# The two long convolutions of each layer: transforms folded by token parity and by mirrored frequency

## What is computed

```python
def hyena_filters(L, w1, b1, w2, b2, w3, b3, freq, w_out, deltas):
    ...
    a = jnp.sin(freq * (a @ w3 + b3))
    decay = jnp.exp(-t * jnp.abs(deltas)[None, :])
    h = ((a @ w_out) * decay).astype(jnp.float32).reshape(L, N_DIRS, HYENA_ORDER, D_HYENA)
    fwd, bwd = h[:, 0], h[:, 1]
    two_sided = jnp.concatenate(
        [fwd, jnp.zeros((1, HYENA_ORDER, D_HYENA), jnp.float32), bwd[:0:-1]], axis=0)
    return jnp.fft.rfft(two_sided, axis=0)

def fft_long_conv(u, h_f, bias):
    L = u.shape[1]
    u32 = u.astype(jnp.float32)
    y = jnp.fft.irfft(jnp.fft.rfft(u32, n=2 * L, axis=1) * h_f[None], n=2 * L, axis=1)[:, :L]
    return (y + u32 * bias.astype(jnp.float32)).astype(u.dtype)
...
        z = fft_long_conv(hv, filt[:, 0], flt_bias[l, 0]) * hx1
        z = fft_long_conv(z, filt[:, 1], flt_bias[l, 1]) * hx2
        y_h = z * jax.nn.silu(z_h)
```

## Time and profile before

| | us |
|---|---|
| median of 3 runs (2068.70 to 2070.05) | 2069.11 |
| the profiled execution | 2067.41 |
| its span, first to last instruction | 2065.6 |
| TensorE busy in it | 1998.3 (97%) |
| VectorE busy | 659.8 (32%) |
| ScalarE busy | 379.0 (18%) |
| mean granted TensorE clock | 0.985 |

### The profile page before, as it was taken

The page is one execution under the profiler, slowest core; times in us unless marked ns, Lnnn a source line. Parts: engine busy times, 40 slices in busy tenths (PEclk is TensorE's granted clock), DMA queues, the critical chain, the costliest instruction groups (busy, mean ns, idle before and its releaser), DMA issues.

```text
span 2065.6 us, 28841 instructions
## 1 busy us (share of the span) xinstructions
PE 1998.3 (97%) x12128; PEld 1104.6 (53%) x12128; DVE 659.8 (32%) x1436; ACT 379.0 (18%) x784; POOL 111.1 (5%) x94
## 2 busy tenths in 40 slices
PE   6999999999998999999989988999999999999998
PEld 5577775667774865777756544232323333333332
DVE  3265113345212474344449934010101010111112
ACT  3212103212102232243320012010101010111101
POOL 0000000000000000000016610000000000000000
PEclk9999999999999999999999998999999999999999
DMA  8245575344665223243323125989898979797973
GB/s 316 82 163 204 217 282 202 116 156 171 234 265 228 82 82 150 115 175 131 123 102 123 41 102 217 376 329 374 324 384 330 381 309 403 311 402 298 406 299 148
DMA packets 41645, 472.71 MB, mean 229 GB/s; under 512 B 4676, under 2 KB 6340, under 8 KB 8040
## 3 DMA queue, kind: packets, MB, share of 16 engines
q1 hardware_dynamic: 39008, 465.44, 56.6%
q10 hardware_dynamic: 2568, 6.31, 0.9%
HBM read 470.68 MB, written 1.06 MB: 228 GB/s over the span
## 4 chain that ended last, share of the span: by engine, by line
PE 88%; DVE 7%; DMA 3%; issue 1%; ACT 0%; ACTq 0%; SPq 0%; POOLq 0%; POOL 0%; DVEq 0%
PE bank L898 21%; PE bank L551 14%; PE bank L928 11%; PE bank L850 7%; PE bank L862 3%; PE bank L714 3%; PE bank L543 3%; PE bank L536 3%; PE bank L720 3%; PE bank L564 2%; PE bank L978 2%; PE bank L970 2%; DMA arena<-in_wgu 1%; PE bank L617 1%; PE bank L649 1%; PE bank L1074 1%
## 5 line engine op out<-in xcount | busy, mean ns | idle before, releaser
L898 PE MATMUL bank<-arena 128*32 128x512 f32 x4096 | 453.1, 594 | 1.7 <-DMA arena<-in_wgu 1.7
L551 PE MATMUL bank<-arena 128*128 128x256 f32 x1408 | 312.6, 381 | 0.0
L898 PEld LDWEIGHTS bank<-arena 128*32 128x32 f32 x4096 | 130.3, 110 | 311.1 <-issue 296.3
L551 PEld LDWEIGHTS bank<-arena 128*128 128x128 f32 x1408 | 264.9, 190 | 53.7 <-issue 19.4
L928 PE MATMUL bank<-arena 128*32 128x512 f32 x2112 | 238.2, 595 | 0.0
L1993 DVE TENSOR_TENSOR arena<-arena,bank 128x256 f32<-128x256 f32 x64 | 27.0, 421 | 595.3 <-ACT arena L1406 540.4
L850 PE MATMUL bank<-arena 128*128 128x256 f32 x704 | 153.7, 379 | 0.1
L850 PEld LDWEIGHTS bank<-arena 128*128 128x128 f32 x704 | 133.6, 190 | 21.7 <-issue 4.1
L928 PEld LDWEIGHTS bank<-arena 128*32 128x32 f32 x2112 | 63.0, 110 | 133.2 <-issue 132.5
L1406 ACT ACTIVATE arena<-bank 128x256 f32<-128x256 f32 x64 | 24.5, 383 | 587.9 <-PE bank L898 587.9
L2207 POOL TENSOR_TENSOR arena<-arena 128x512 f32<-128x512 f32 x64 | 81.2, 1268 | 293.0 <-DVE arena L2040 290.5
(11 more groups left out here) (416 smaller groups left out, 1952.6 us busy)
## 6 DMA issues: line engine op xcount, KB each, us to landing
arena<-in_wgu SPq DMA_DIRECT2D x88, 2048.0 KB, 9.4
arena<-in_w SPq DMA_DIRECT2D x46, 2048.0 KB, 8.1
arena<-in_wdn SPq DMA_DIRECT2D x88, 1024.0 KB, 7.9
arena<-in_modw SPq DMA_DIRECT2D x24, 2048.0 KB, 10.2
arena<-in_wf SPq DMA_DIRECT2D x11, 3072.0 KB, 10.3
arena<-in_flt_deltas ACTq DMA_DIRECT2D x2, 1024.0 KB, 15.6
cst<-in_consts SPq DMA_DIRECT2D x1, 1162.0 KB, 17.3
arena<-in_x SPq DMA_DIRECT2D x1, 1024.0 KB, 5.3
```

The lines of the kernel that those rows point to most:

```text
L551: ins = mm(bank[b][:, j * S:(j + 1) * S], w[:, col:col + P], hT[:, k, :], start=(k == 0), stop=(k == KT - 1))
L898: ins = mm(bank[w % 2][32 * j:32 * j + 32, :], hTe[:, k, TOK * b:TOK * b + TOK], wslot[c % RING][:, k, :], start=(k == 0), stop=(k == KT - ...
```

## The change

Of the 256 frequencies only the lower 128 are transformed, once over the even tokens and once over the odd tokens. At the mirrored frequency the cosine of an even token is the same and that of an odd token has its sign turned, and the sine the other way round; so the upper half is a difference where the lower is a sum.

- The constants are reordered: rows of tokens by parity, and the inverse's rows mirrored. The decay's times, the columns of `fa` and of the transposes' source are taken with a step of two.
- "f_spec": 4 matmuls of 128x512 for each order, not 8. ScalarE copies two of the four banks, and VectorE makes sum and difference with the other two: 4 instructions for each order.
- "dft": 2 matmuls of 128x512 for each half, not 4; the second accumulates onto the first. ScalarE copies the first's two banks aside (`even`, signalled as du_ready), the matmuls of the second step wait for that and no longer for VectorE. VectorE does nothing in the first step; in the second it does both halves' six instructions, two that make the upper half (`2 * even - sum`), and four sums over `Y` for the inverse: 18 in a row.
- "idft": 16 matmuls of 128x128, not 128x256, with the constants read in steps of two elements; VectorE reads the bank de-interleaved.
- The table moves the "dft" steps behind "mix", and "turn" and "idft" of both orders one place later.
- Three waits are merged into others: filter_landed for delta_landed and fwo_landed, mask_landed for ffw_landed, ScalarE's own chain for two of its waits.

```diff
         7: [("dft", 0, 0), ("scores", 0, 0)],
-        8: [("dft", 0, 1), ("mix", 0, 0)],
-        9: [("weigh", 0, 0), ("idft", 0, 0), ("scores", 1, 0)],
-        10: [("turn", 1, 0), ("mix", 1, 0), ("values", 0, 0)],
-        11: [("weigh", 1, 0), ("dft", 1, 0), ("scores", 2, 0)],
-        12: [("dft", 1, 1), ("mix", 2, 0), ("values", 1, 0)],
-        13: [("weigh", 2, 0), ("scores", 3, 0)],
+        8: [("mix", 0, 0), ("dft", 0, 1)],
+        9: [("weigh", 0, 0), ("scores", 1, 0)],
+        10: [("mix", 1, 0), ("idft", 0, 0), ("values", 0, 0)],
+        11: [("weigh", 1, 0), ("turn", 1, 0), ("scores", 2, 0)],
+        12: [("mix", 2, 0), ("dft", 1, 0), ("values", 1, 0)],
+        13: [("weigh", 2, 0), ("dft", 1, 1), ("scores", 3, 0)],
         14: [("mix", 3, 0), ("values", 2, 0)],
-        15: [("weigh", 3, 0), ("idft", 1, 0)],
-        16: [("values", 3, 0)],
+        15: [("weigh", 3, 0)],
+        16: [("values", 3, 0), ("idft", 1, 0)],
...
                     elif name == "f_spec":
 
                         pe.wait_ge(sm["fold_ready"], l + 1)
-                        for kt in range(2):
+                        if c == 1:
+                            pe.wait_ge(sm["fp_done"], l * 4 + 2)
+                        for t in range(TT):
                             for ri in range(2):
-                                q = 2 * kt + ri
-                                if c == 1:
-                                    pe.wait_ge(sm["fp_done"], l * 8 + q + 1)
-                                for t in range(TT):
-                                    lhs = (FCt, FSt)[ri][:, t, kt * P:(kt + 1) * P]
-                                    rhs = hf[:, t, c, :] if ri == 0 else hn[:, t, c, :]
-                                    ins = mm(bank[4 + q][:, :], lhs, rhs, start=(t == 0), stop=(t == TT - 1))
-                                ins.then_inc(sm["fp_ps"], 1)
+                                src = (hf, hn)[ri][:, t, c, :]
+                                mm(bank[4 + 2 * t + ri][:, :], (FCt, FSt)[ri][:, t, 0:P], src,
+                                   start=True, stop=True).then_inc(sm["fp_ps"], 1)
...
                                 ins = nc.tensor.transpose(bank[2 + t][:, j * P:(j + 1) * P],
-                                                          src[:, j, t * P:(t + 1) * P], ident)
+                                                          src[:, j, t::2], ident)
...
 
                         if h == 0:
                             pe.wait_ge(sm["utok_ready"], l * 4 + 2 * c + 2)
                         else:
-                            pe.wait_ge(sm["spec_ready"], l * 4 + 2 * c + 1)
+                            pe.wait_ge(sm["du_ready"], l * 4 + 2 * c + 2)
                         for ri in range(2):
-                            for t in range(TT):
-                                ins = mm(bank[2 + ri][:, :], (FCt, FSt)[ri][:, t, h * P:(h + 1) * P], utok[:, t, :],
-                                         start=(t == 0), stop=(t == TT - 1))
+                            ins = mm(bank[2 + ri][:, :], (FCt, FSt)[ri][:, h, 0:P], utok[:, h, :],
+                                     start=(h == 0), stop=True, skip_group_check=True)
                         ins.then_inc(sm["dft_ps"], 1)
                     elif name == "idft":
 
                         pe.wait_ge(sm["spec_ready"], l * 4 + 2 * c + 2)
                         for j in range(4):
-                            for kt in range(2):
+                            for t in range(TT):
+                                at = (j % 2) * S + t * P
                                 for ri in range(2):
-                                    ins = mm(bank[2 + j // 2][:, (j % 2) * S:(j % 2 + 1) * S],
-                                             Y[:, kt, ri, j * P:(j + 1) * P], (FCk, FSk)[ri][:, kt, :],
-                                             start=(kt == 0 and ri == 0), stop=(kt == 1 and ri == 1))
+                                    ins = mm(bank[2 + j // 2][:, at:at + P], H[:, c, t, ri, j * P:(j + 1) * P],
+                                             (FCk, FSk)[ri][:, 0, t::2], start=(ri == 0), stop=(ri == 1))
...
-                        for q in range(4):
-                            act.wait_ge(sm["fp_ps"], l * 8 + 4 * c + q + 1)
-                            F(H[:, c, q // 2, q % 2, :], bank[4 + q][:, :], ACT.Copy).then_inc(sm["fp_done"], 1)
+                        for ri in range(2):
+                            act.wait_ge(sm["fp_ps"], l * 8 + 4 * c + ri + 1)
+                            F(H[:, c, 1, ri, :], bank[4 + ri][:, :], ACT.Copy).then_inc(sm["fh_ready"], 1)
+                    elif name == "dft" and h == 0:
+                        act.wait_ge(sm["dft_ps"], l * 4 + 2 * c + 1)
+                        for ri in range(2):
+                            F(even[:, ri, :], bank[2 + ri][:, :], ACT.Copy).then_inc(sm["du_ready"], 1)
...
-                        if c == 0 and h == 0:
-                            dve.wait_ge(sm["fp_done"], l * 8 + 8)
-                        dve.wait_ge(sm["dft_ps"], l * 4 + 2 * c + h + 1)
-                        C, Sn = bank[2][:, :], bank[3][:, :]
-                        re, im = H[:, c, h, 0, :], H[:, c, h, 1, :]
-                        link(v.tensor_tensor(tmp[:, 0, :], C, re, ALU.mult))
-                        link(v.tensor_tensor(tmp[:, 1, :], Sn, im, ALU.mult))
-                        link(v.tensor_tensor(Y[:, h, 0, :], tmp[:, 0, :], tmp[:, 1, :], ALU.add))
-                        link(v.tensor_tensor(tmp[:, 0, :], Sn, re, ALU.mult))
-                        link(v.tensor_tensor(tmp[:, 1, :], C, im, ALU.mult))
-                        v.tensor_tensor(Y[:, h, 1, :], tmp[:, 0, :], tmp[:, 1, :], ALU.subtract).then_inc(sm["spec_ready"], 1)
-                        dve.wait_ge(sm["spec_ready"], l * 4 + 2 * c + h + 1)
+                        if h == 0:
+                            continue
+                        dve.wait_ge(sm["du_ready"], l * 4 + 2 * c + 2)
+                        dve.wait_ge(sm["dft_ps"], l * 4 + 2 * c + 2)
+                        for half in range(2):
+                            re, im = H[:, c, half, 0, :], H[:, c, half, 1, :]
+                            if half == 0:
+                                C, Sn = bank[2][:, :], bank[3][:, :]
+                            else:
+
+                                C, Sn = even[:, 0, :], even[:, 1, :]
+                                link(v.scalar_tensor_tensor(C, C, 2.0, bank[2][:, :], ALU.mult, ALU.subtract))
+                                link(v.scalar_tensor_tensor(Sn, Sn, -2.0, bank[3][:, :], ALU.mult, ALU.add))
+                            link(v.tensor_tensor(tmp[:, 0, :], C, re, ALU.mult))
+                            link(v.tensor_tensor(tmp[:, 1, :], Sn, im, ALU.mult))
+                            link(v.tensor_tensor(Y[:, half, 0, :], tmp[:, 0, :], tmp[:, 1, :], ALU.add))
+                            link(v.tensor_tensor(tmp[:, 0, :], Sn, re, ALU.mult))
+                            link(v.tensor_tensor(tmp[:, 1, :], C, im, ALU.mult))
+                            link(v.tensor_tensor(Y[:, half, 1, :], tmp[:, 0, :], tmp[:, 1, :], ALU.subtract))
+                        for ri in range(2):
+                            for t in range(TT):
+                                ins = v.tensor_tensor(H[:, c, t, ri, :], Y[:, 0, ri, :], Y[:, 1, ri, :],
+                                                      ALU.add if ri == t else ALU.subtract)
+                                if t == 0:
+                                    link(ins)
+                            ins.then_inc(sm["spec_ready"], 1)
+                            dve.wait_ge(sm["spec_ready"], l * 4 + 2 * c + ri + 1)
+                    elif name == "f_spec":
+                        for ri in range(2):
+                            dve.wait_ge(sm["fh_ready"], l * 4 + 2 * c + ri + 1)
+                            dve.wait_ge(sm["fp_ps"], l * 8 + 4 * c + 2 + ri + 1)
+                            whole, alias, odd = H[:, c, 0, ri, :], H[:, c, 1, ri, :], bank[6 + ri][:, :]
+                            link(v.tensor_tensor(whole, alias, odd, ALU.add))
+                            ab = (alias, odd) if ri == 0 else (odd, alias)
+                            v.tensor_tensor(alias, ab[0], ab[1], ALU.subtract).then_inc(sm["fp_done"], 1)
+                            dve.wait_ge(sm["fp_done"], l * 4 + 2 * c + ri + 1)
                     elif name == "idft":
                         u, gate = (hvT, hx1T) if c == 0 else (hx1T, hx2T)
                         if c == 1:
@@ -1615,9 +1638,11 @@
                         for b in range(2):
                             dve.wait_ge(sm["idft_ps"], l * 4 + 2 * c + b + 1)
                             for j in (2 * b, 2 * b + 1):
-                                link(v.scalar_tensor_tensor(tmp[:, 0, 0:S], u[:, j, :],
+                                turned = bank[2 + b][:, (j % 2) * S:(j % 2 + 1) * S]
```

(9 more changed lines are left out.)

43 lines of the change are left out of this document (20 added, 23 removed).

## The result

The changed kernel takes 2077.73 us (median of 20 runs), the kernel before 2071.43 us beside it (20 runs): a ratio of 1.0028, with a 95% interval of 1.0019 to 1.0038. It is slower by 0.3%, some 6 us, where 4.9 were forecast. Its profiled execution took 2076.88 us, its span 2074.9.

What follows compares the result with a forecast made beforehand. TensorE was taken as the bound, so saved matmuls count unless it waits. Matmuls -41.6, waits +37.2 and half clock +9.3 gave +4.9 us: 2074.0 us against a median of 2069.1, range 2069.5 to 2080.

Steps and rivals of the forecast that it cites:

- The matmuls saved: Filter spectra, forward transforms and inverses on TensorE: 20.8 us less a layer, 41.6 in both.
- What I took at nothing: Hidden spectra sums, `even` copies, merged waits, strided operands and weight loads: forecast to add no time.
- The three-operand form: VectorE's two instructions making the upper half in the second "dft" step: 0.75 us each at 512, 1.58 together with gaps.
- The waits: TensorE standing for banks whose release is delayed by VectorE's 18 instructions, twice a layer: 18.6 us a layer, 37.2 in both.
- place one: First order: the 18 stand ahead of reading HX1's second half, so TensorE waits 10.1 us before HX2, each layer.
- place two: Second order: the 18 delay head 3's scores and ScalarE's modmul copy; TensorE waits 8.5 us before ZH's second half.
- The clock: TensorE at half clock behind each of four long waits: 2.3 us each, 9.3 in all (5.9 to 12.4).
- TensorE's busy time: Forecast to fall by some 32 us, not 41.6, because half clock makes matmuls longer.
- Rival one: Clock returns soon: 2.93 us at half clock per wait, 5.9 in all; 2070.6 us, not measurably slower; chance 0.33.
- Rival five: A further unseen wait, such as VectorE-GpSimd contention or slower de-interleaved reading: 2 to 4 us, 2077; chance 0.04.
- Rivals two, three and four: Two: waits, full clock, 2064.7 (0.03); three: no waits, 2027.5 (0.05); four: strided inverse operand at half rate, 2087.8 (0.07).

## Why the prediction was right, point by point

The mechanism, the places and the side were right, and the forecast of +4.9 us stands against 6.3 between the medians and 5.2 to 6.2 in the stretch. That the sum came so close is in part luck, as its terms show. Term by term, both layers together:

- **The matmuls saved**, 41.6 forecast. By starts, summed over the stretch, the spectra went from 27.67 to 13.95 us, the transforms from 27.85 to 14.13, the inverse from 28.00 to 14.51: 40.9. The busy time by line of the two kernels (line, shapes, count, busy us, mean ns of one record) shows the same:

```profile
L640 PE MATMUL bank<-arena,cst 128*128 128x512 f32 x64 | 28.8, 592 | 0.0
L617 PE MATMUL bank<-arena,cst 128*128 128x512 f32 x64 | 28.3, 595 | 0.0
L649 PE MATMUL bank<-cst,arena 128*128 128x256 f32 x128 | 28.3, 379 | 0.0
...
L629 PE MATMUL bank<-cst,arena 128*128 128x128 f32 x24 | 3.2, 275 | 0.0
```

```profile
L552 PE MATMUL bank<-arena 128*128 128x256 f32 x1217 | 279.4, 390 | 36.5 <-DVE arena L1546 20.1 <-ACT arena L1234 16.5
...
L647 PE MATMUL bank<-cst,arena 128*128 128x128 f32 x128 | 15.2, 275 | 0.0
L637 PE MATMUL bank<-arena,cst 128*128 128x512 f32 x32 | 15.0, 592 | 0.0
L615 PE MATMUL bank<-arena,cst 128*128 128x512 f32 x32 | 14.6, 599 | 0.0
...
L627 PE MATMUL bank<-cst,arena 128*128 128x128 f32 x24 | 3.5, 287 | 0.0
```

- **What I took at nothing.** The sums for the filter were hidden, as forecast: TensorE has no wait there. The step of two in the inverse's constants costs 0.24. The transposes that read their source with a step of two I had also put at nothing, and that was a small miss: L629 with 275 ns is L627 with 287, and by starts the 24 took 3.16 us where they took 2.67, so 0.5. (No run takes the step out of the transposes alone, so that it is the step is argued.)
- **The three-operand form** was guessed at 0.75 us for 128x512; it takes 0.69 (L1608 in the timeline of VectorE above), no more than the plain one. The block of 18 took 130.81 - 117.74 = 13.07 and not 13.2.
- **The waits**, 10.1 and 8.5 forecast: 10.03 and 8.22. The walk for place one reads 134.06 - 111.89 = 22.2 us from the end of HX1's first half (22.3 forecast), of which TensorE fills 12.1 (12.2). For place two it reads 197.11 - 177.91 = 19.2 (19.4). Sum 36.5 and not 37.2.
- **The clock**, 9.3 forecast, with 5.9 to 12.4 as its bounds: 8.0 in the first profile, 9.0 in the second. Behind all twenty long waits of six profiles it was 2.3 us on average (1.5 to 3.0), the value taken from the earlier trace rows. The rule of the Trainium skill cited there ("TensorE: Matmul & The Clock Gate", "HAM oscillation — how this bites in real kernels") names the cost rightly: at 134.06 the mean clock of 0.75 over 9.24 us is 4.6 us at half clock, half of which is 2.3, and the group took 2.2 longer. The run with idle matmuls shows the cost by itself.
- **The sum in the stretch**: -40.9 + 0.5 (transposes) + 36.5 + 8.9 (all projections, by starts: 266.27 to 275.20) + 0.2 (small differences of other lines) = +5.2, measured +5.2. Forecast +4.9. The savings were sized 0.7 too large, the small items 0.7 too small, the waits 0.7 and the clock 0.4 too large. Of the 8.9, though, only 8.0 stand behind the four new waits, so the clock's term was 1.3 too large there; the other 0.9 came in the two parts that every kernel has, where one kernel differs from itself by up to 1.7. The errors cancelled.
- **TensorE's busy time** was to fall by 32. In the stretch it fell by 604.62 - 573.26 = 31.4, the 40.9 less 8.9 of half clock and 0.7 of small items; in the whole program by 30.0.
- **The rivals.** Rival one had its point of decision at 4.2 us of half clock for each wait. The first profile's 8.0 us are 2.0 for each, so half clock for 4.0: just under the point, on the rival's side. The second's 9.0 are 4.5, on the forecast's side. That the stretch is 5.2 us longer all the same, and not under the 4.1 that can be told, is due to the 1.4 us that savings and small items came out short, and to the 0.9 just named. The sign hung on a microsecond or two, and the chance of 0.33 for no measurable change was not too high. Rival five's further wait does exist, for in_w in the third layer, but at a place that the change doesn't touch, and it comes and goes. Rivals two, three and four are excluded by the four groups at 0.71 to 0.83 of the clock, by the waits, and by 3.63 us for the inverse.

## What to carry to other kernels

When matmuls are replaced by elementwise sums, count how many of these stand in one row on their engine, and what is read out of a bank behind them: here VectorE was busy for a third of the time, and four rows of 13 us (36.5 us of waits and 8.0 to 9.0 of clock) cost more than the 41 us saved. Before giving up such a change, move the row: the same arithmetic, hung where every bank's reading behind it still comes in time, turned +0.3% into -2%. And price a wait of the engine that bounds the kernel with what its clock does behind it: for the four waits of the changed kernel that was 8.0 and 9.0 us, and it decided the sign.

## What the runs showed of the hardware

- The clock's cost is nearly the same after 5.3 us of standing (2.8 and 3.0) as after 10.0 (1.5 to 3.0). After 3.0 to 3.1 us it was 1.7 twice and nothing twice, in one execution, with the same work on both sides.
- Shorter waits can cost it as well, behind other work: the one for bias_rows cost 1.6 us in all seven profiles in which it was 1.86 to 2.31 us long, and nothing in the four in which it was 1.52 to 1.81. Waits of 0.4 and 0.5 us, in the run with 11 and 9 idle matmuls, cost nothing at four places, nor did those of 0.92 to 0.95 us before line 536, 24 times in twelve profiles (7.03 to 7.04 us behind each).
- Matmuls that compute nothing of use keep the clock up: 7.01 us behind them at four places out of four.
- A three-operand instruction of VectorE on 128x512 takes 0.69 us, as long as one with two operands, where at 128x256 it took 0.48 against 0.42.
- A moving operand read with a step of two float32 elements costs 0.06 us in 3.6; eight transposes with a source in steps of two took 0.16 us more in 0.9, which no run isolates.
